# Mixing expert sizes in one group: 25 groups of four 32-place units in the first expert layer

## The chip, the cores and the metric

The kernel runs on one core of one Trainium2 chip. The metric is the device time of one execution in microseconds. Matrix products run on TensorE, element-wise work on VectorE (DVE) and ScalarE (ACT), set-up work on GpSimd (POOL), and SyncE (SP) issues nearly all DMA transfers.

## The reference, cut to what matters

Two blocks of a network follow each other on 256 rows (tokens) of 1024 numbers. Each block ends in a mixture of experts; only the first one's is touched. It has 64 experts, and every row goes to the eight with the highest scores:

```python
s = jax.nn.sigmoid((hf @ w_router).astype(jnp.float32))
_, idx = lax.top_k(s + b_router.astype(jnp.float32), TOP_K)        # TOP_K = 8 of 64
s_sel = jnp.take_along_axis(s, idx, axis=-1)
wts = s_sel / jnp.sum(s_sel, axis=-1, keepdims=True) * ROUTE_SCALE
# for the rows of each expert e, with rw the weight of row and expert:
y = (jax.nn.silu(xb @ we_gate[e]) * (xb @ we_up[e])) @ we_down[e]  # 1024 -> 256 -> 1024
acc = acc.at[rows].add(y * rw[:, None])
```

A shared expert is added for all rows. All numbers are float32, and each expert has 3 MB of weights, 1 MB for each of gate, up and down.

## The kernel before

**Groups.** The experts with numbers 0 to 3 keep places of their own, and the other 60 are sorted by their number of rows, most first, so that position 4 has most rows and position 63 fewest. A group fills the 128 output rows of TensorE with one, two or four experts of equal capacity: 128, 64 or 32 places. There are 26 groups (lines 42 to 55): the four unsorted experts by twos, then eight times one group of one or two, one of two and one of four. An expert with more rows than its capacity would be worked off by another path after the last group (`over_items`); it loads that expert's weights again.

**One group on TensorE** (`experts`, `body`, lines 1207 to 1265; the matmul helpers record lines 1215, 1228, 1246, 1251, 1361 and 1374). It is written out in this order: gate and up of group g (line 1361, for each of 8 steps over the 1024 inputs one matmul for each expert of the group; an expert's matmul uses only the columns of the array that are its places, so a group of two has tiles 128 rows by 64 columns and a group of four 128 by 32); the combine of group g-1 (line 1228, four float32 products that add the group's output rows to the tokens' rows in PSUM banks 0 to 3); transposes of the activation (line 1246) and of the weighted selection `Sw` (line 1251); the gather of group g+1 (line 1215, 48 bfloat16 products of the input, held as three bfloat16 parts, with the 0/1 selection `Sb`); down of group g (line 1374, two steps, two halves of 512 columns).

**The other engines.** VectorE makes the selection `Sb` and its weighted form `Sw` for group g+1 (lines 1974 and 1978), multiplies Silu(gate) by up (line 1990) and copies the two transposed blocks (lines 1993 and 1995). ScalarE takes Silu (line 779), copies the gathered rows (line 774), and after down copies the output rows to `Y` (line 785), which the combine waits for by the semaphore `x_Y`.

**The weights.** They come through a ring of 12 slots of 1 MB in the order in which TensorE needs them (`PIECES1`, line 60: for each group the gates, then the ups, then the downs). SP issues a piece when the piece 12 places before it has been used (line 497 waits, line 499 issues). The sorted experts' pieces also need the list of the sort, which is read before each issue. Float32 products are two records each in the trace (a weight load and a matmul, twice), bfloat16 ones one.

**What follows.** After the last combine come the norm and the second block, with a second expert layer (lines 1508 and 1520) of 8 groups of four experts, all 32 places. It shares the function `experts` and is not changed.

Of the kernel before, what the change touches and what calls it, by code (L numbers as in the profile page):

```python
# [33 lines left out]
G2 = 4  # L34
# [2 lines left out]

STATIC1 = 4  # L40
GROUPS1 = [(0, 2), (2, 2)]
_one, _two, _four = 4, 8, 32
for _t in range(8):
    if _t % 2 == 0:
        GROUPS1.append((_one, 1))
        _one += 1
    else:
        GROUPS1.append((_two, 2))
        _two += 2
    GROUPS1.append((_two, 2))  # L50
    _two += 2
    GROUPS1.append((_four, 4))
    _four += 4
assert (_one, _two, _four) == (8, 32, 64)
NG1 = len(GROUPS1)

SLOTS, SLOT_WORDS, RING0 = 12, 2048, 0
PIECES1 = [(-1, kind, 0) for kind in range(3)] + [(g, kind, j) for g, (_, n) in enumerate(GROUPS1) for kind in range(3) for j in range(n)]  # L60
# [90 lines left out]
def two_block_network(nc, A, out):  # L151
# [10 lines left out]
    with ctx:  # L162
# [136 lines left out]
        av = ce(512)  # L299
        aT = ce(4, P)  # L300
        Y = ce(D)
        mask = ce(NB, E1)
        wts = ce(NB, E1)
        rank = ce(NB, E1)
# [95 lines left out]
        def _(sp):  # L400
# [82 lines left out]
            def load_piece(i):  # L483

                g, kind, j = piece = PIECES1[i]
                slot = RING[piece][0]
                if i >= SLOTS:
                    consumed(PIECES1[i - SLOTS])
                else:

                    sp.wait_ge(S["stream_used"], AT[("adb4", "adb5", "w_out")[slot // 4]] + 1)
                if g < 0:
                    src = A[("ws_gate", "ws_up", "ws_down")[kind]][0]
                    src = rows(src) if kind == 2 else long_rows(src, KD)
                else:
                    at = GROUPS1[g][0] + j
# [162 lines left out]
        def _(act):  # L659
# [105 lines left out]
            def experts(L, NG, F, GU):  # L765
# [100 lines left out]
        def _(pe):  # L866
# [340 lines left out]
            def experts(L, NG, F, gate_and_up, down):  # L1207
                before = (L - 1) * NG1

                def gather_rows(done):  # L1210

                    for k in range(KD):
                        for q in range(NB * 3):
                            b, part = q // 3, q % 3
                            last = mm(PS[4 + k // 4][:, (k % 4) * P:(k % 4 + 1) * P], hs[:, part, b, k * P:(k + 1) * P],  # L1215
                                      Sb[:, b, :], start=(q == 0), stop=(q == NB * 3 - 1))
                        if k % 4 == 3:
                            last.then_inc(done, 1)

                def gather(n):  # L1220
                    pe.wait_ge(S["x_S"], 2 * (n + before) + 2)
                    gather_rows(S["x_gather"])

                def add_rows():

# [5 lines left out]

                def combine(g):
                    pe.wait_ge(S["x_Ct"], (g + before) + 1)
                    pe.wait_ge(S["x_Y"], 2 * (g + before) + 2)
                    return add_rows()

                def body(g, par, first=False, last=False):

                    pe.wait_ge(S["x_hTe"], 2 * (g + before) + 2)
                    gate_and_up(g)  # L1240
                    if not first:
                        combine(g - 1)

                    pe.wait_ge(S["x_act"], (g + before) + 1)
                    for f in range(F // P):
                        m = tr(PS[6][:, f * P:(f + 1) * P], av[:, f * P:(f + 1) * P], ident[:])  # L1246
                    m.then_inc(S["x_turned"], 1)
                    if first:
                        pe.wait_ge(S["over_known"], L)
                    for b in range(NB):  # L1250
                        m = tr(PS[7][:, b * P:(b + 1) * P], Sw[:, par, b, :], ident[:])
                    m.then_inc(S["x_turned"], 1)
                    if not last:
                        gather(g + 1)
# [7 lines left out]
                gather(0)  # L1262
                if L == 1:
                    shared_down()
                over_list(L)
# [85 lines left out]

            def gate_and_up1(g):

                n = GROUPS1[g][1]
                cap = P // n
                for kind in range(2):
                    for j in range(n):
                        landed((g, kind, j))
                    for k in range(KD):
                        for j in range(n):  # L1360
                            m = mm(PS[4 + kind][j * cap:(j + 1) * cap, 0:F1], hTe[:, k, j * cap:(j + 1) * cap],  # L1361
                                   piece_view((g, kind, j))[:, k, :], start=(k == 0), stop=(k == KD - 1))
                    m.then_inc(S["e1_gateup"], 1)

            def down1(g):

                n = GROUPS1[g][1]
                cap = P // n
                for j in range(n):
                    landed((g, 2, j))  # L1370
                for c in range(F1 // P):
                    for h in range(2):
                        for j in range(n):
                            m = mm(PS[6 + h][j * cap:(j + 1) * cap, :], aT[:, c, j * cap:(j + 1) * cap],  # L1374
                                   piece_view((g, 2, j))[:, c, h * 512:(h + 1) * 512], start=(c == 0), stop=(c == F1 // P - 1))
                m.then_inc(S["e1_down"], 1)

# [150 lines left out]
        def _(dve):  # L1528
# [362 lines left out]
            def over_rows(L, ne):  # L1891
# [6 lines left out]
                    step(v.memset(over_from, float(CAP2)))  # L1898
                else:

                    step(v.tensor_scalar(over_from, over_idx, 32.5, 32.0, ALU.is_lt, ALU.mult))
                    step(v.tensor_scalar(over_from, over_from, 32.0, None, ALU.add))
                    for bound, rows in ((8.5, 64.0), (4.5, -64.0)):
# [62 lines left out]
            def experts(L, NG, F, GU):  # L1966
                pre, before = f"e{L}_", (L - 1) * NG1

                def slots(n, par):

                    first, G = GROUPS1[n] if L == 1 else (n * G2, G2)
                    cap = P // G
                    for b in range(NB):
                        v.tensor_tensor(Sb[:, b, :].rearrange("p (e s) -> p e s", e=G), outer(iota[:, 0:cap], G),  # L1974
                                        inner(rank[:, b, bass.ds(first, G)], cap), ALU.is_equal).then_inc(S["x_S"], 1)
                    dve.wait_ge(S["x_S"], 2 * (n + before) + 2)
                    for b in range(NB):
                        v.tensor_tensor(Sw[:, par, b, :].rearrange("p (e s) -> p e s", e=G),
                                        Sb[:, b, :].rearrange("p (e s) -> p e s", e=G),
                                        inner(wts[:, b, bass.ds(first, G)], cap), ALU.mult).then_inc(S["x_Sw"], 1)  # L1980

                def body(g, par, last=False):
                    dve.wait_ge(S["x_Sw"], 2 * (g + before) + 2)
                    if not last:
# [5 lines left out]
                    v.tensor_tensor(av[:, 0:F].rearrange("s (c p) -> s p c", p=P), sg[:, 0:F].rearrange("s (p c) -> s p c", p=P),  # L1990
                                    PS[5][:, 0:F].rearrange("s (p c) -> s p c", p=P), ALU.mult).then_inc(S["x_act"], 1)
# [3 lines left out]
                    v.tensor_copy(Ct, PS[7][:, 0:T]).then_inc(S["x_Ct"], 1)  # L1995
# [5 lines left out]
                if L == 1:  # L2001
                    for g in range(NG):
                        body(g, g % 2, last=g == NG - 1)
                else:
                    body(0, 0)
                    with dve.Fori(0, NG // 2 - 1) as i:
# [241 lines left out]
```

## Time and profile before

| | |
|---|---|
| three runs | 1555.62, 1557.53, 1557.55 us; median 1557.53 |
| the profiled execution, first to last instruction | 1555.2 us |
| the profiled execution's time around it | no other time is shown; the span stands 2.3 us below the median of the runs |
| TensorE busy (matmul) | 1255.3 us, 81% |
| VectorE, ScalarE, GpSimd busy | 360.8, 178.9, 95.2 us |
| transfers | 507.48 MB, mean 326 GB/s |
| mean granted TensorE clock | 0.908 of full speed |
| first expert layer, first gate matmul to end of last combine | 324.5 to 810.2 us |

The profile records one execution. "Busy" counts the time in which an engine works on an instruction; TensorE matmuls overlap each other, and their ends are modelled, so starts say more than durations. The chain of waits is followed back from the last instruction: at each step to what released it, or to the instruction before it on its engine. Its pieces show what the end of the kernel hung on at each moment. "issue" is time without a wait that the profile shows.

### The profile page before, as it was taken

The page shows a single profiled execution, that of the slowest core. Times are in us where ns is not written, and L with a number is a line of the kernel's source. Part 1 is how long each engine was busy: PE and PEld are TensorE (multiplying, and loading weights), DVE is VectorE, ACT ScalarE, POOL GpSimd, SP SyncE. Part 2 cuts the span into 40 slices and gives each one's busy share as a digit, 9 for nine tenths or more (in the row PEclk, how much of TensorE's full clock was granted, in tenths as well). Part 3 has the DMA queues.
Part 4 walks back from the last instruction along what each step waited for, and adds up shares of the span by engine and source line. Part 5 has one row for each costly group of instructions (what it writes and reads, how often), then busy time and mean ns, then how long its engine had stood idle before and what let it go on. Part 6 is the DMA issues. An engine that isn't in the chain of part 4 may idle for free.

```text
span 1555.2 us, 19875 instructions
## 1 busy us (share of the span) xinstructions
PE 1255.3 (81%) x8092; PEld 644.6 (41%) x8092; DVE 360.8 (23%) x877; ACT 178.9 (12%) x340; POOL 95.2 (6%) x125
## 2 busy tenths in 40 slices
PE   4999889799989989989977988887565765765754
PEld 2763435456556556555536544433221221221211
DVE  1588452611111111111113243324000000000002
ACT  1210200311111111111110012012000000000001
POOL 2595000000000000000001000000000000000000
PEclk9999979999999999999997999998886887887787
DMA  9765992278999999999976412363999999999993
GB/s 364 274 273 212 397 413 106 97 265 320 380 420 420 420 420 421 420 421 418 421 306 221 170 47 108 145 272 123 423 421 421 421 422 421 422 422 422 422 422 141
DMA packets 83877, 507.48 MB, mean 326 GB/s; under 512 B 8262, under 2 KB 9510, under 8 KB 34260
## 3 DMA queue, kind: packets, MB, share of 16 engines
q1 hardware_dynamic: 82708, 502.98, 79.3%
q0 software_dynamic: 944, 3.29, 0.7%
q8 instruction: 58, 0.95, 0.2%
q14 instruction: 23, 0.19, 0.0%
q10 hardware_dynamic: 144, 0.07, 0.0%
HBM read 505.25 MB, written 1.06 MB: 326 GB/s over the span
## 4 chain that ended last, share of the span: by engine, by line
PE 56%; DMA 33%; DVE 6%; SPq 2%; issue 1%; ACT 1%; DVEq 0%; ACTq 0%
DMA W<-in_w_expert_down 12%; DMA W<-in_w_expert_up 10%; PE PS L1361 10%; DMA W<-in_we_up 8%; PE PS L936 5%; PE PS L1228 5%; PE PS L1374 4%; PE PS L1430 4%; PE PS L1215 3%; PE PS L1508 3%; PE PS L1520 3%; DMA W<-in_w_ada 3%; PE PS L890 2%; PE PS L1101 2%; PE PS L1390 2%; PE PS L1488 2%
## 5 line engine op out<-in xcount | busy, mean ns | idle before, releaser
L1508 PE MATMUL PS<-W,scr 128*32 128x512 f32 x1024 | 175.6, 850 | 130.6 <-DMA W<-in_w_expert_up 66.8
L1361 PE MATMUL PS<-W,scr 128*32 128x256 f32 (+2 forms) x2048 | 195.6, 399 | 24.5 <-DMA W<-in_we_up 22.7
L1990 DVE TENSOR_TENSOR scr<-scr,PS 128x256 f32<-128x256 f32 (+1 forms) x34 | 24.1, 708 | 670.5 <-PE PS L1508 387.1
L1361 PEld LDWEIGHTS PS<-W,scr 128*32 128x32 f32 (+2 forms) x2048 | 126.5, 132 | 101.7 <-issue 53.4
L1508 PEld LDWEIGHTS PS<-W,scr 128*32 128x32 f32 x1024 | 40.3, 148 | 265.1 <-issue 112.8
L1228 PE MATMUL PS<-scr 128*128 128x512 f32 x272 | 125.3, 603 | 2.6 <-ACT scr L785 2.6
L1520 PE MATMUL PS<-W,scr 128*32 128x512 f32 x512 | 71.2, 706 | 34.2 <-DMA W<-in_w_expert_down 33.2
L1215 PE MATMUL PS<-scr 128*128 128x128 bf16 x1632 | 96.7, 219 | 0.4 <-DVE scr L1974 0.4
L1374 PE MATMUL PS<-W,scr 128*32 128x512 f32 (+2 forms) x512 | 94.9, 597 | 0.7 <-DVE scr L1993 0.7
L1215 PEld LDWEIGHTS PS<-scr 128*128 128x128 bf16 x1632 | 93.9, 98 | 2.1 <-DVE scr L1945 1.2
L774 ACT COPY scr<-PS 128x512 f32<-128x512 f32 x68 | 39.9, 587 | 436.7 <-PE PS L1215 436.7
L1228 PEld LDWEIGHTS PS<-scr 128*128 128x128 f32 x272 | 49.2, 189 | 68.2 <-issue 68.0
L890 PE MATMUL PS<-W,sc 128*32 128x512 f32 x384 | 49.2, 658 | 18.1 <-DMA W<-in_w_ada 17.9
L785 ACT COPY scr<-PS 128x512 f32<-128x512 f32 x68 | 36.5, 589 | 217.9 <-PE PS L1520 125.3
L1430 PE MATMUL PS<-W,hT 128*128 128x512 f32 x128 | 57.1, 599 | 0.0
L1520 PEld LDWEIGHTS PS<-W,scr 128*32 128x32 f32 x512 | 17.6, 127 | 80.7 <-DMA W<-in_w_expert_down 40.2
L936 PE MATMUL PS<-hT,W 128*128 128x256 f32 x192 | 44.1, 392 | 4.5 <-DVE hT L1570 4.5
L1374 PEld LDWEIGHTS PS<-W,scr 128*32 128x32 f32 (+2 forms) x512 | 28.3, 126 | 47.0 <-issue 43.9
L632 POOL TENSOR_SCALAR scr<-scr,convw 128x256 f32<-128x256 f32 x44 | 44.2, 1004 | 4.3
L936 PEld LDWEIGHTS PS<-hT,W 128*128 128x128 f32 x192 | 37.6, 197 | 10.0 <-DVE hT L1570 4.6
L779 ACT ACTIVATE scr<-PS 128x256 f32<-128x256 f32 (+1 forms) x34 | 14.8, 434 | 219.9 <-PE PS L1508 142.2
L1993 DVE COPY scr<-PS 128x256 f32<-128x256 f32 (+1 forms) x34 | 16.6, 488 | 100.3 <-PE PS L1246 100.3
(411 smaller groups left out, 1111.3 us busy)
## 6 DMA issues: line engine op xcount, KB each, us to landing
W<-in_we_gate SPq DMA_DIRECT2D x64, 1024.0 KB, 19.1
W<-in_we_up SPq DMA_DIRECT2D x64, 1024.0 KB, 17.0
W<-in_we_down SPq DMA_DIRECT2D x64, 1024.0 KB, 16.0
W<-in_w_expert_gate SPq DMA_DIRECT2D x64, 1024.0 KB, 18.7
W<-in_w_expert_up SPq DMA_DIRECT2D x64, 1024.0 KB, 19.3
W<-in_w_expert_down SPq DMA_DIRECT2D x64, 1024.0 KB, 19.4
W<-in_w_ada SPq DMA_DIRECT2D x12, 4096.0 KB, 18.1
W<-in_w_in SPq DMA_DIRECT2D x6, 4096.0 KB, 14.4
```

What stands on the lines that cost most here:

```text
L632: step(g.tensor_scalar(tmp, upad[:, i, :, j:j + ROW], convw[:, 4 * j + i:4 * j + i + 1], None, ALU.mult))
L774: a.copy(hTe[:, 4 * q:4 * q + 4, :], PS[4 + q][:].rearrange("p (k s) -> p k s", k=4)).then_inc(S["x_hTe"], 1)
L785: a.copy(Y[:, h * 512:(h + 1) * 512], PS[6 + h][:]).then_inc(S["x_Y"], 1)
L890: last = mm(PS[5 + h][32 * j:32 * j + 32, :], sc[:, 2 * j + kk, 30 - row:62 - row], ada_w[n][:, 2 * j + kk, h * 512:(h + 1) * 512], start= ...
L936: last = mm(PS[bank][:, at:at + n], lhs(k), rhs(k), start=(k == 0), stop=(k == KD - 1))
L1215: last = mm(PS[4 + k // 4][:, (k % 4) * P:(k % 4 + 1) * P], hs[:, part, b, k * P:(k + 1) * P], Sb[:, b, :], start=(q == 0), stop=(q == NB ...
L1228: last = mm(PS[2 * b + h][:, :], Ct[:, b * P:(b + 1) * P], Y[:, h * 512:(h + 1) * 512], start=False, stop=False)
L1361: m = mm(PS[4 + kind][j * cap:(j + 1) * cap, 0:F1], hTe[:, k, j * cap:(j + 1) * cap], piece_view((g, kind, j))[:, k, :], start=(k == 0), s ...
L1374: m = mm(PS[6 + h][j * cap:(j + 1) * cap, :], aT[:, c, j * cap:(j + 1) * cap], piece_view((g, 2, j))[:, c, h * 512:(h + 1) * 512], start=( ...
L1430: last = mm(PS[6 + n % 2][:, :], hT[:, k, b * P:(b + 1) * P], w2k[2 + half][:, k, h * 512:(h + 1) * 512], start=(k == 0), stop=(k == KD - 1))
L1508: m = mm(PS[bank][j * CAP2:(j + 1) * CAP2, :], hTe[:, k, j * CAP2:(j + 1) * CAP2], gu2[piece][:, j, kk, :], start=(k == 0), stop=(k == KD ...
L1520: m = mm(PS[6 + h][j * CAP2:(j + 1) * CAP2, :], aT[:, c, j * CAP2:(j + 1) * CAP2], dn2[piece][:, j, cc, h * 512:(h + 1) * 512], start=(c = ...
```

## The change

The first layer's groups are built of four units of 32 places. A group is a list of (position, units): the unsorted experts keep two units each; positions 4 to 7 have three units (96 places instead of 128), 8 to 31 two and 32 to 63 one, as before. 14 groups take one expert of two units and two of one; 4 take one of three and one of one; 5, besides the first two, take two of two. That makes 25. An expert of three units is computed as a tile of 64 columns and one of 32 with the same weights (`column_tiles`).

The combine's matmuls become bfloat16: the selection's transposed form holds 0 and 1 (`CtB`), and the output rows are split into three bfloat16 parts (`Y3`) by ScalarE and VectorE in turns (`parts_of_rows`). The routing weight goes into the activation: TensorE adds up each place's weight into one column of PSUM bank 5, and VectorE's multiplication of gate and up takes it as a third factor. The selection is double-buffered (`Sb2`).

```diff
+UNIT = 32
+WIDE1, HALF1 = 8, 32
+def first_layer_groups():
+    groups = [[(0, 2), (1, 2)], [(2, 2), (3, 2)]]
+    wide, half, single = STATIC1, WIDE1, HALF1
+    for t in range(14):
+        groups.append([(half, 2), (single, 1), (single + 1, 1)])
+        half, single = half + 1, single + 2
+        if t % 3 == 1 and wide < WIDE1:
+            groups.append([(wide, 3), (single, 1)])
+            wide, single = wide + 1, single + 1
+        elif t % 3 == 2 or t == 13:
+            groups.append([(half, 2), (half + 1, 2)])
+            half += 2
+    return groups
+def column_tiles(group):
+    for j, (_, at, cap) in enumerate(places(group)):
+        for size in (2 * UNIT, UNIT):
+            if cap >= size:
+                yield j, at, size
+                at, cap = at + size, cap - size
...
 # ScalarE, experts, body
+                    if L == 1:
+                        for h in range(2):
+                            a.copy(Y3[:, 0, h * 512:(h + 1) * 512], PS[6 + h][:]).then_inc(S["x_Y"], 1)
+                        for h in range(2):
+                            act.wait_ge(S["x_rest"], 4 * g + 1 + h)
+                            a.copy(Y3[:, 1, h * 512:(h + 1) * 512], Yr[:, h * 512:(h + 1) * 512]).then_inc(S["x_Y"], 1)
+                        return
...
 # TensorE, combine
+                    pe.wait_ge(S["x_Y"], 4 * g + 4)
+                    pe.wait_ge(S["x_rest"], 4 * g + 4)
+                    for b in range(NB):
+                        for part in range(3):
+                            for h in range(2):
+                                m = mm(PS[2 * b + h][:, :], CtB[:, b * P:(b + 1) * P], Y3[:, part, h * 512:(h + 1) * 512],
+                                       start=False, stop=False)
...
 # TensorE, body
+                    if L == 1:
+                        pe.wait_ge(S["x_Sw"], 2 * g + 2)
+                        for b in range(NB):
+                            mm(PS[5][:, F:F + 1], Sw[:, par, b, :], ones[:, 0:1], start=(b == 0), stop=(b == NB - 1))
                     gate_and_up(g)
...
-                        m = tr(PS[7][:, b * P:(b + 1) * P], Sw[:, par, b, :], ident[:])
+                            m = mm(PS[7][:, b * P:(b + 1) * P], Sb2[:, par, b, :], identb, start=True, stop=True)
...
 # TensorE, gate_and_up1 (down1 likewise)
                     for k in range(KD):
-                        for j in range(n):
-                            m = mm(PS[4 + kind][j * cap:(j + 1) * cap, 0:F1], hTe[:, k, j * cap:(j + 1) * cap],
+                        for j, at, size in column_tiles(GROUPS1[g]):
+                            m = mm(PS[4 + kind][at:at + size, 0:F1], hTe[:, k, at:at + size],
                                    piece_view((g, kind, j))[:, k, :], start=(k == 0), stop=(k == KD - 1))
...
 # VectorE, body
+                        v.scalar_tensor_tensor(out=av[:, 0:F]..., in0=sg[:, 0:F]...,
+                                               scalar=PS[5][:, F:F + 1], in1=PS[5][:, 0:F]...,
+                                               op0=ALU.mult, op1=ALU.mult).then_inc(S["x_act"], 1)
...
+                def parts_of_rows(g):
+                    for h in range(2):
+                        q = slice(h * 512, (h + 1) * 512)
+                        dve.wait_ge(S["x_Y"], 4 * g + 1 + h)
+                        v.tensor_tensor(Yr[:, q], PS[6 + h][:], Y3[:, 0, q], ALU.subtract).then_inc(S["x_rest"], 1)
+                    for h in range(2):
+                        q = slice(h * 512, (h + 1) * 512)
+                        dve.wait_ge(S["x_Y"], 4 * g + 3 + h)
+                        v.tensor_tensor(Y3[:, 2, q], Yr[:, q], Y3[:, 1, q], ALU.subtract).then_inc(S["x_rest"], 1)
```

The selection on VectorE (`slots`) is made in one operation for each run of experts of equal size, so a mixed group takes two operations where a uniform one takes one, for each of two blocks and of two forms.

## Rows read from the trace of the kernel before

**Rows 1.** The page's 40 slices of 38.9 us: GB/s moved in each.

```profile
GB/s 364 274 273 212 397 413 106 97 265 320 380 420 420 420 420 421 420 421 418 421 306 221 170 47 108 145 272 123 423 421 421 421 422 421 422 422 422 422 422 141
```

**Rows 2.** Sums by stretch: busy time (and count) of each engine, clock, DMA share, GB/s.

```profile
355.00:397.00 42.00, 42.00 (x360) 26.34 (x360) 4.70 (x14) 6.72 (x13) 0.00 (x0) 1.00 0.75 289
397.00:797.00 400.00, 375.52 (x3405) 224.22 (x3394) 48.36 (x144) 55.27 (x105) 0.00 (x0) 0.97 1.01 419
```

**Rows 3.** Chain of waits, a group of two, then one of four: start, duration, what.

```profile
373.67 7.06 PE PS L1361 x64
380.72 3.63 PE PS L1228 x8
384.36 0.22 PE PS L1246 x2
...
384.79 2.68 PE PS L1215 x48
387.47 3.58 PE PS L1374 x16
391.06 7.04 PE PS L1361 x128
...
408.42 3.60 PE PS L1361 x31
```

**Rows 4.** Chain of waits where the first group begins.

```profile
324.31 0.22 PE PS L1205 x2
324.53 7.08 PE PS L1361 x64
```

**Rows 5.** Chain of waits in the last group, from its transposes on.

```profile
800.72 0.44 DVE scr L1993
...
801.57 3.67 PE PS L1374 x32
...
806.49 3.67 PE PS L1228 x8
```

**Rows 6.** Groups by form, 290 to 860 us: busy, mean ns | idle before.

```profile
L1974 DVE TENSOR_TENSOR scr<-iota,scr 128x128 bf16<-128x128 f32 x52 | 12.8, 289 | 53.2 <-PE PS L1215 53.1
...
L1882 DVE TENSOR_TENSOR xn<-PS,scr 128x512 f32<-128x512 f32 x4 | 2.5, 683 | 0.0
...
L763 ACT CAST scr<-xn 128x512 bf16<-128x512 f32 x4 | 2.4, 618 | 2.0 <-DVE xn L1882 2.0
```

**Rows 7.** TensorE timeline, last round of down and first of gate: start, duration, what.

```profile
338.69 0.60 PE L1374 MATMUL PS<-W,scr 128*64 128x512 f32 x2
339.12 0.60 PE L1361 MATMUL PS<-W,scr 128*64 128x256 f32 x4
...
390.46 0.60 PE L1374 MATMUL PS<-W,scr 128*64 128x512 f32 x2
390.99 0.42 PE L1361 MATMUL PS<-W,scr 128*32 128x256 f32 x4
...
407.81 0.61 PE L1374 MATMUL PS<-W,scr 128*32 128x512 f32 x4
408.35 0.44 PE L1361 MATMUL PS<-W,scr 128*64 128x256 f32 x2
```

**Rows 8.** TensorE timeline, the second rounds of gate after the last two borders.

```profile
391.23 0.40 PE L1361 MATMUL PS<-W,scr 128*32 128x256 f32 x4
...
408.62 0.39 PE L1361 MATMUL PS<-W,scr 128*64 128x256 f32 x2
```

**Rows 9.** TensorE timeline, down after the gather: first and second round.

```profile
387.40 0.65 PE L1374 MATMUL PS<-W,scr 128*64 128x512 f32 x2
...
387.88 0.60 PE L1374 MATMUL PS<-W,scr 128*64 128x512 f32 x2
...
404.78 0.64 PE L1374 MATMUL PS<-W,scr 128*32 128x512 f32 x4
...
405.23 0.61 PE L1374 MATMUL PS<-W,scr 128*32 128x512 f32 x4
```

More of the change, by code:

```diff
@@ L36, with places @@
 NG2 = E2 // G2
+UNIT = 32
 STATIC1 = 4
[L41 to L54, printed above, removed]
-NG1 = len(GROUPS1)
+WIDE1, HALF1 = 8, 32
[11 more added lines that the diff above has]
+            half += 2
+    assert (wide, half, single) == (WIDE1, HALF1, E1), (wide, half, single)
+    return groups
+GROUPS1 = first_layer_groups()
+NG1 = len(GROUPS1)
+def places(group):
+    start = 0
+    for position, units in group:
+        yield position, start * UNIT, units * UNIT
+        start += units
+def column_tiles(group):
[4 more added lines that the diff above has]
+                at, cap = at + size, cap - size
 SLOTS, SLOT_WORDS, RING0 = 12, 2048, 0
-PIECES1 = [(-1, kind, 0) for kind in range(3)] + [(g, kind, j) for g, (_, n) in enumerate(GROUPS1) for kind in range(3) for j in range(n)]
+PIECES1 = [(-1, kind, 0) for kind in range(3)] + [(g, kind, j) for g, group in enumerate(GROUPS1) for kind in range(3) for j in range(len(group))]
 RING = {piece: ((RING0 + i) % SLOTS, i // SLOTS) for i, piece in enumerate(PIECES1)}
@@ L301, in two_block_network @@
         Y = ce(D)
+        Y3 = ce(3, D, dt=BF16)
+        Yr = ce(D)
+        Sb2 = ce(2, NB, P, dt=BF16)
+        CtB = ce(T, dt=BF16)
+        identb = ce(P, dt=BF16)
         mask = ce(NB, E1)
@@ L1215, in gather_rows, with gather @@
                             last = mm(PS[4 + k // 4][:, (k % 4) * P:(k % 4 + 1) * P], hs[:, part, b, k * P:(k + 1) * P],
-                                      Sb[:, b, :], start=(q == 0), stop=(q == NB * 3 - 1))
+                                      pick[:, b, :], start=(q == 0), stop=(q == NB * 3 - 1))
                         if k % 4 == 3:
                             last.then_inc(done, 1)
-                def gather(n):
+                def gather(n, par):
                     pe.wait_ge(S["x_S"], 2 * (n + before) + 2)
-                    gather_rows(S["x_gather"])
+                    gather_rows(S["x_gather"], Sb2[:, par, :, :] if L == 1 else Sb)
                 def add_rows():
@@ L1250, in body @@
                     for b in range(NB):
[L1251 removed]
+                        if L == 1:
+                            m = mm(PS[7][:, b * P:(b + 1) * P], Sb2[:, par, b, :], identb, start=True, stop=True)
+                        else:
+                            m = tr(PS[7][:, b * P:(b + 1) * P], Sw[:, par, b, :], ident[:])
                     m.then_inc(S["x_turned"], 1)
                     if not last:
[L1254 removed]
+                        gather(g + 1, 1 - par)
                     pe.wait_ge(S["x_aT"], (g + before) + 1)
@@ L1261, in experts @@
                 pe.wait_ge(S["hs_left"], 8 * L)
-                gather(0)
+                gather(0, 0)
                 if L == 1:
@@ L1365, in down1 @@
             def down1(g):
-                n = GROUPS1[g][1]
-                cap = P // n
-                for j in range(n):
+                for j in range(len(GROUPS1[g])):
                     landed((g, 2, j))
@@ L1372, in down1 @@
                     for h in range(2):
-                        for j in range(n):
-                            m = mm(PS[6 + h][j * cap:(j + 1) * cap, :], aT[:, c, j * cap:(j + 1) * cap],
+                        for j, at, size in column_tiles(GROUPS1[g]):
+                            m = mm(PS[6 + h][at:at + size, :], aT[:, c, at:at + size],
                                    piece_view((g, 2, j))[:, c, h * 512:(h + 1) * 512], start=(c == 0), stop=(c == F1 // P - 1))
@@ L1899, in over_rows @@
                 else:
-                    step(v.tensor_scalar(over_from, over_idx, 32.5, 32.0, ALU.is_lt, ALU.mult))
-                    step(v.tensor_scalar(over_from, over_from, 32.0, None, ALU.add))
-                    for bound, rows in ((8.5, 64.0), (4.5, -64.0)):
+                    step(v.tensor_scalar(over_from, over_idx, HALF1 + 0.5, float(UNIT), ALU.is_lt, ALU.mult))
+                    step(v.tensor_scalar(over_from, over_from, float(UNIT), None, ALU.add))
+                    for bound, rows in ((WIDE1 + 0.5, float(UNIT)), (STATIC1 + 0.5, -float(UNIT))):
                         step(v.tensor_scalar(cap_tmp, over_idx, bound, rows, ALU.is_lt, ALU.mult))
@@ L1969, in slots @@
                 def slots(n, par):
-                    first, G = GROUPS1[n] if L == 1 else (n * G2, G2)
-                    cap = P // G
+                    if L == 1:
+                        parts = []
+                        for first, at, cap in places(GROUPS1[n]):
+                            if parts and parts[-1][3] == cap and parts[-1][0] + parts[-1][1] == first:
+                                parts[-1][1] += 1
+                            else:
+                                parts.append([first, 1, at, cap])
+                    else:
+                        parts = [[n * G2, G2, 0, CAP2]]
+                    pick = Sb2[:, par, :, :] if L == 1 else Sb
                     for b in range(NB):
-                        v.tensor_tensor(Sb[:, b, :].rearrange("p (e s) -> p e s", e=G), outer(iota[:, 0:cap], G),
-                                        inner(rank[:, b, bass.ds(first, G)], cap), ALU.is_equal).then_inc(S["x_S"], 1)
+                        for first, G, at, cap in parts:
+                            ins = v.tensor_tensor(pick[:, b, at:at + G * cap].rearrange("p (e s) -> p e s", e=G), outer(iota[:, 0:cap], G),
+                                                  inner(rank[:, b, bass.ds(first, G)], cap), ALU.is_equal)
+                        ins.then_inc(S["x_S"], 1)
                     dve.wait_ge(S["x_S"], 2 * (n + before) + 2)
                     for b in range(NB):
-                        v.tensor_tensor(Sw[:, par, b, :].rearrange("p (e s) -> p e s", e=G),
-                                        Sb[:, b, :].rearrange("p (e s) -> p e s", e=G),
-                                        inner(wts[:, b, bass.ds(first, G)], cap), ALU.mult).then_inc(S["x_Sw"], 1)
+                        for first, G, at, cap in parts:
+                            ins = v.tensor_tensor(Sw[:, par, b, at:at + G * cap].rearrange("p (e s) -> p e s", e=G),
+                                                  pick[:, b, at:at + G * cap].rearrange("p (e s) -> p e s", e=G),
+                                                  inner(wts[:, b, bass.ds(first, G)], cap), ALU.mult)
+                        ins.then_inc(S["x_Sw"], 1)
                 def body(g, par, last=False):
@@ L2001, in experts @@
                 if L == 1:
+                    step(v.tensor_copy(identb, ident[:]))
                     for g in range(NG):
                         body(g, g % 2, last=g == NG - 1)
+                        parts_of_rows(g)
                 else:
```

24 lines of the change are left out of this document (14 added, 10 removed).

## The prediction

> **What bounds the kernel now.** I read the 40 slices of the page first, then sums by stretch over the first expert layer, then the chain of waits at its start, in its middle and at its end, and last single tensor matmuls where one tile width follows another. The 40 slices show two stretches at 420 GB/s, one in each expert layer [rows 1]. In the first layer, 324.5 to 810 us, the sums by stretch show that from 397 to 797 the weights stream at 419 GB/s, while TensorE is busy 375.5 of 400 us; from 355 to 397 TensorE is busy all the time and the DMAs move only 289 GB/s [rows 2]. So the layer is bound by TensorE for its first 70 us and by the stream of weights after that, but TensorE has little to spare: the chain gives one group of experts 17.4 us (373.67 to 391.06, and 391.06 to 408.42), whatever its number of experts [rows 3]. It is the reserve that this change spends: 26 groups of 17.4 us are 452 us of the 485 us that the layer takes.
>
> **The parts of a group.** In the chain a group is: gate and up 7.05, combine 3.63, four transposes 0.44, gather 2.68, down 3.58 [rows 3].
>
> Combine. Four float32 products of 512 columns (8 records, 3.63) become twelve bfloat16 ones. The gather is 48 bfloat16 records of 128 columns, 6144 columns in 2.68 us; twelve of 512 are 6144 columns too: 2.68. Minus 0.95.
>
> Turning the selection. Two float32 transposes of the weights (0.22) become two bfloat16 products of 128 columns, 2/48 of the gather's time (0.11). Minus 0.1.
>
> Weight per row. Two new float32 products with one column are 4 records with 128x128 weights each. One such product of 36 columns, 2 records, takes 0.22 us in the chain just before the first group [rows 4], so two take 0.44. They also put full-width work between two tiled stages, which costs a change of width more (below, 0.10). I take plus 0.6; the ends are 0.4 and 0.9.
>
> The multiplication on VectorE reads one more scalar. It stands beside the combine, and what waits for it (the transposes) stands behind the combine on TensorE anyway: it costs nothing up to 2.68 us, and the VectorE operations of up to 128x512 take 0.3 to 0.7 us [rows 6]. In the first group, without a combine, it could cost 0.1. The copies of the transposed blocks stand beside the gather as before: 0. So does the one new conversion of the identity, once. The loads come in another order on SP, each with its wait and its issue as before, 192 of them: 0 while the ring is full.
>
> Three parts of the rows. In the last group down ends at 805.24 (801.57 + 3.67) and the combine starts at 806.49, 1.25 us for two halves copied by ScalarE [rows 5]. Now it is copy, subtract, cast, subtract, in halves. Neighbours: a subtraction of 128x512 from PSUM 683 ns, a bfloat16 cast 618 ns [rows 6]. Pipelined over halves it is about 0.6+0.7+0.7+0.6+0.7 with waits, 3.9 us. Combine comes after the next group's gate and up (7 us), so in the 24 inner places it is covered. Behind it on VectorE stands the next selection, up to 8 operations of at most 0.29 us [rows 6]: 3.9+2.3 is 6.2, still below 7, and the up product is awaited anyhow. TensorE's combine has a longer wait, for the subtractions too, and behind it are the transposes into the banks that these read; both come after it anyway. On ScalarE the next Silu stands behind the casts; it needs the next gate, 3.5 us later, and can be 0 to 1 us late, under cover of up. Only the last group pays: 3.9 instead of 1.25, plus 2.7.
>
> Sum for a group of one tile width: 17.4 - 0.95 - 0.1 + 0.6 = 16.95 us.
>
> **The mixed groups.** 18 of the 25 groups (14 of three experts, 4 with a 96-place one) issue, for each of 8 steps of gate and of up, a 64-wide tile and two 32-wide tiles, and so for each of 4 steps of down. Before, a group has tiles of one width only. The trace shows what a change of width costs at stage borders. From 64 to 64 wide, the last 512-column round starts at 338.69 and the next stage at 339.12: 0.43, the length of the round. From 64 to 32 wide it is 390.46 to 390.99, from 32 to 64 wide 407.81 to 408.35, thus 0.53 and 0.54 [rows 7]. A change costs 0.10 us, in either direction. The first round after it is longer as well: a 256-column round starts its follower after 0.24 (390.99 to 391.23, 32 wide) or 0.27 (408.35 to 408.62, 64 wide) [rows 8], where 32 rounds in 7.05 us are 0.22 each; of 512 columns, 387.40 to 387.88 is 0.48 and 404.78 to 405.23 is 0.45 [rows 9], against 0.43. No new-width matmul starts while one of the old width runs. That is the point: four tiles of one width share a round (four 32-wide ones start within it), but here every round would hold one width.
>
> I take it that the new width waits for the old one's end even where the columns are disjoint. Each float32 product is two rounds. One step of gate or up is then 64 wide 0.27 + 0.22 + 0.10 minus rounding (0.58), 32 wide 0.24 + 0.22 + 0.10 minus rounding (0.55): 1.13 us instead of 0.43. Sixteen steps: 18.1 instead of 6.9, plus 11.2. One step of down: 0.48 + 0.53 + 0.45 + 0.53 less rounding, 1.98 instead of 0.86; four steps: 7.9 instead of 3.5, plus 4.4. A mixed group takes 16.95 + 15.6 = 32.55 us.
>
> Its bounds: below, the widths overlap at no cost (plus 0); above, the passes alternate between the widths, eight changes a step pair instead of four, 1.25 us a step and 20 us for gate and up, 8.4 for down: plus 18, 35 us.
>
> The Trainium skill, TensorEngine Tiling (Array Packing), Key Properties, says the same more strongly: changing the tiling mode, not just the tile, drains the engine. The 0.10 us agrees, and a drain means no overlap of the two widths; the trace has no pair of widths on disjoint columns, so no row shows that half. By the rule the sum is the one above; without it, it would be that of the first rival.
>
> **Sum of the layer.** 18 x 32.55 = 585.9, 7 x 16.95 = 118.7, together 704.6. The first group has no combine of its predecessor (-2.7), the last gathers nothing (-2.7) and waits 0.9 for its transposed rows (800.72 to 801.57 [rows 5]), and then come 3.9 and the last combine 2.7: 706.7 us. From 324.53 [rows 4] the layer ends at 1031, where the last combine ended at 810.2 before [rows 5]: plus 221. The weights don't hold this up: three experts are 9 transfers of 1.05 MB, 22.5 us at 419 GB/s [rows 2], below 32.55, and the ring of 12 pieces is refilled a group ahead. What follows (the block after it, the second expert layer, whose code is unchanged) moves back as a whole. The profiled execution's span is 1555.2 us, 2.3 below the median of 1557.53; I add the difference to the median: 1557.5 + 221 = 1778.5, rounded to 1778 us.
>
> **Rivals.**
> 1. Faster: widths on disjoint columns share the array and a change costs nothing. For it: tiles of one width do run side by side, four 32-wide ones in the time of one. Against it: the 0.10 us at every change. Then every group takes 16.95, and the stream binds. The first sorted groups hold three experts instead of one, two and four, so the ring is emptied sooner: the stretch 355 to 397 was short of 419 GB/s by 130 x 42 us = 5.5 MB, 5.2 transfers or 13 us [rows 2]. Less 2.7 for the longer tail: minus 10, 1547 us. It holds as long as TensorE is faster than the stream: 180 sorted transfers at 2.5 us are 450 us, less 118.7 for the seven others leaves 18.4 us for each mixed group. Its own ends are 0 and minus 13, without the tail.
> 2. Little change, slower by about 1%: a change costs its 0.10 us and the slower first round, but disjoint tiles overlap. A step is 0.43 + 0.20 + 0.05, 0.68 us; gate and up 10.9, down 4.4: plus 4.9, 21.8 a mixed group. 18 x 21.8 + 118.7 = 511, plus 2.1, from 324.5 to 838: plus 27, 1585 us. It sits between one and the forecast.
> 3. The new chain of four steps is the bound (VectorE or ScalarE late for combine in each group). By the sum above it is 6.2 of 7 us; if it took 9, 7 unmixed groups would lose 2 us each and, without the slow mixed tiles, hidden behind the stream. It is worth at most 14 us and needs rival 1 to be seen.
> 4. It doesn't do what it says: an expert beyond 96 places would go the overflow way. That way loads the expert again; the sign of it would be more transfers of gate weights than there are experts; each such expert would add a whole pass of gather, gate, up and down after the last group, 17 us and its loads, and the prediction would be short by that.
>
> **Chances.** Forecast 0.82, rival 1 0.10, rival 2 0.05, the rest 0.03. The forecast's own range is 1745 to 1850: 18 groups at 31 to 36 us. For other splits of the rounds I widen it downwards, to 1690 to 1850. A measurement of this kernel can tell 0.2% (3 us) from no change: faster 0.09, within it 0.03, slower 0.88.
>
> **What would show it.** Gate and up of a mixed group at 18 us and down at 8 in the chain, starts of 64- and 32-wide matmuls never in one round; the share of DMA in the chain of the first layer gone and its rate near 300 GB/s; combine 2.7 us, ready before gate and up end; unmixed groups at 17 us. It is wrong if mixed gate and up stays near 7 us with DMA waits as before.

## The result and the profile after

The changed kernel takes 1777.35 us (median of 4 runs, 1775.53 to 1778.05), the kernel before 1556.6 (4 runs); the ratio is 1.1411, 95% interval 1.1397 to 1.1424. The forecast was 1778 us. The profiled execution took 1777.13 us with a span of 1775.4, 220.2 more than the span before.

The chain of waits through the second group (two experts, one width) and the third (three experts, two widths); start, duration, what. L1412 is gate and up, L1279 combine, L1296 the first transposes, L1252 gather, L1423 down, L1289 the weight for each row:

```profile
341.81 0.54 PE PS L1289 x4
342.35 7.06 PE PS L1412 x64
...
349.56 2.54 PE PS L1279 x11
...
355.11 3.58 PE PS L1423 x16
358.69 0.54 PE PS L1289 x4
359.23 18.11 PE PS L1412 x96
...
377.50 2.54 PE PS L1279 x11
380.03 0.22 PE PS L1296 x2
...
380.36 2.68 PE PS L1252 x48
383.04 7.94 PE PS L1423 x24
390.98 0.54 PE PS L1289 x4
```

They answer to [rows 3]. A group of one width lasts 16.88 us (341.81 to 358.69), a mixed one 32.29 (358.69 to 390.98). Gate and up of the mixed group take 18.11 us for 96 records; the uniform group of four before took 7.04 for 128.

The TensorE timeline of the first steps of that gate shows why. Each row is a query of a short window (20 to 130 ns) that begins after one start, so the row's start is that of the earliest matmul still running, and its count includes any that start within the window:

```profile
359.16 0.43 PE L1412 MATMUL PS<-W,scr 128*64 128x256 f32 x1
...
359.43 0.38 PE L1412 MATMUL PS<-W,scr 128*64 128x256 f32 x1
...
359.74 0.62 PE L1412 MATMUL PS<-W,scr 128*32 128x256 f32 x4
...
359.98 0.39 PE L1412 MATMUL PS<-W,scr 128*32 128x256 f32 x2
...
360.29 0.43 PE L1412 MATMUL PS<-W,scr 128*64 128x256 f32 x1
```

The 64-wide product's two rounds start at 359.16 and 359.43, the first round of the two 32-wide products at 359.74, their second at 359.98, the next 64-wide one at 360.29. No round holds both widths, although their columns are disjoint; the intervals are 0.27, 0.31, 0.24 and 0.31, together 1.13 us a step. (This goes by starts. The modelled end of the 64-wide round, 359.43 + 0.38, lies 0.07 us behind the next start, as the ends do at the borders in [rows 7].)

Sums by stretch (busy time and count of each engine, clock, DMA share, GB/s), to be held against [rows 2]:

```profile
355.00:397.00 42.00, 41.84 (x239) 14.70 (x238) 8.94 (x27) 6.73 (x12) 0.00 (x0) 1.00 0.76 300
397.00:797.00 400.00, 397.77 (x2469) 154.82 (x2481) 67.97 (x186) 51.72 (x95) 0.00 (x0) 1.00 0.71 280
```

The stream of weights no longer binds: 280 GB/s where it was 419, and TensorE is busy 397.8 of 400 us. The end of the layer, to be held against [rows 5]:

```profile
1018.84 3.67 PE PS L1423 x16
1022.53 0.59 ACT scr L816
1023.15 0.70 DVE scr L2068
1023.87 0.62 ACT scr L819
1024.52 1.30 DVE scr L2072 x2
...
1025.96 4.44 PE PS L1279 x12
1030.40 1.81 issue
1032.20 0.40 PE PS L1359
```

Where the 220.2 us are: the layer, from its first gate to the end of the last combine, lasts 703.3 us (327.10 to 1030.40) instead of 485.6, plus 217.7. 2.1 came before it, nearly all of it where the chain's first product of the kernel took 5.65 us instead of 3.69, in code that isn't touched. 0.4 is the first weight column. From the end of the last combine on both need 745.0 us; the 1.81 us of issue behind the combine are within that, and smaller differences later make up for them.

### The profile page after: what moved, and what is told of

The parts are those of the page before. It is cut to its first block, busy times and chain, and to the rows that moved or that the text cites. A ratio compares the mean times of both kernels' runs of the same rounds, so it can differ in the third digit from the quotient of the medians.

```text
span 1775.4 us, 20664 instructions
## 1 busy us (share of the span) xinstructions
PE 1497.3 (84%) x8368; PEld 647.0 (36%) x8392; DVE 427.9 (24%) x1043; ACT 206.7 (12%) x385; POOL 95.2 (5%) x125
## 4 chain that ended last, share of the span: by engine, by line
PE 70%; DMA 22%; DVE 5%; issue 1%; SPq 1%; ACT 1%; DVEq 0%; ACTq 0%
PE PS L1412 21%; DMA W<-in_w_expert_down 10%; PE PS L1423 9%; DMA W<-in_w_expert_up 9%; PE PS L973 5%; PE PS L1252 4%; PE PS L1279 4%; PE PS L1479 3%; PE PS L1557 3%; PE PS L1569 2%; DMA W<-in_w_ada 2%; PE PS L927 2%; PE PS L1138 2%; PE PS L1439 2%; PE PS L1537 2%; PE PS L1522 2%
## 5 line engine op out<-in xcount | busy, mean ns | idle before, releaser
L1412 PE MATMUL PS<-W,scr 128*32 128x256 f32 (+1 forms) x2176 | 377.1, 392 | 0.0
L1412 PEld LDWEIGHTS PS<-W,scr 128*32 128x32 f32 (+1 forms) x2176 | 128.0, 121 | 237.5 <-issue 222.0
L1423 PE MATMUL PS<-W,scr 128*64 128x512 f32 (+1 forms) x544 | 169.7, 607 | 0.8 <-DVE scr L2059 0.8
L804 ACT COPY scr<-PS 128x512 f32<-128x512 f32 x66 | 38.7, 587 | 478.1 <-PE PS L1252 478.1
L1252 PE MATMUL PS<-scr 128*128 128x128 bf16 x1584 | 93.8, 219 | 0.0
L1252 PEld LDWEIGHTS PS<-scr 128*128 128x128 bf16 x1584 | 90.1, 98 | 1.4 <-DVE scr L1994 0.8
L2068 DVE TENSOR_TENSOR scr<-PS,scr 128x512 f32<-128x512 f32 x50 | 32.2, 686 | 232.8 <-ACT scr L816 232.8
L2052 DVE SCALAR_TENSOR_TENSOR scr<-scr,PS 128x256 f32<-128x256 f32 x25 | 16.8, 670 | 283.1 <-PE PS L1412 283.1
L1423 PEld LDWEIGHTS PS<-W,scr 128*64 128x64 f32 (+1 forms) x544 | 31.7, 121 | 118.9 <-issue 115.5
L1279 PE MATMUL PS<-scr 128*128 128x512 bf16 x276 | 65.3, 386 | 7.3 <-issue 3.8
L1569 PEld LDWEIGHTS PS<-W,scr 128*32 128x32 f32 x512 | 17.4, 127 | 79.8 <-DMA W<-in_w_expert_down 39.2
L816 ACT CAST scr<-PS 128x512 bf16<-128x512 f32 x50 | 26.9, 589 | 161.1 <-PE PS L1423 161.1
L1279 PEld LDWEIGHTS PS<-scr 128*128 128x128 bf16 x300 | 27.7, 99 | 44.5 <-issue 15.7
```

What stands on the lines that cost most here:

```text
L804: a.copy(hTe[:, 4 * q:4 * q + 4, :], PS[4 + q][:].rearrange("p (k s) -> p k s", k=4)).then_inc(S["x_hTe"], 1)
L1279: m = mm(PS[2 * b + h][:, :], CtB[:, b * P:(b + 1) * P], Y3[:, part, h * 512:(h + 1) * 512], start=False, stop=False)
L1412: m = mm(PS[4 + kind][at:at + size, 0:F1], hTe[:, k, at:at + size], piece_view((g, kind, j))[:, k, :], start=(k == 0), stop=(k == KD - 1))
L1423: m = mm(PS[6 + h][at:at + size, :], aT[:, c, at:at + size], piece_view((g, 2, j))[:, c, h * 512:(h + 1) * 512], start=(c == 0), stop=(c = ...
L1569: m = mm(PS[6 + h][j * CAP2:(j + 1) * CAP2, :], aT[:, c, j * CAP2:(j + 1) * CAP2], dn2[piece][:, j, cc, h * 512:(h + 1) * 512], start=(c = ...
```

## The experiments

**All tiles 32 wide.** The change with one function altered:

```diff
-        for size in (2 * UNIT, UNIT):
-            if cap >= size:
-                yield j, at, size
-                at, cap = at + size, cap - size
+        while cap > 0:
+            yield j, at, UNIT
+            at, cap = at + UNIT, cap - UNIT
```

> All tiles of the first expert layer are 32 wide (an expert of 64 places is two tiles with the same weights), the rest of the change stays. Theory (two widths never share a round, and each change of width costs about 0.1 us more): gate and up of every group 7.1 us, down 3.6, a group 16.9 us of TensorE; then the stream of weights binds and the kernel takes about 1547 us (1543 to 1557), near or below the kernel before. Rival (the mixed groups are slow because a step has more matmuls and weight loads, three or more for a group, and issue can't keep up): four tiles a step are worse than three, gate and up 18 us or more, about 1777 us or above.

Measured: ratio to before 0.9995 (0.9984 to 1.0007), median 1555.62 us. A group of three experts in its chain, from its weight column to the next one's:

```profile
356.24 0.54 PE PS L1288 x4
356.78 7.04 PE PS L1411 x128
...
369.53 3.57 PE PS L1422 x32
373.10 0.54 PE PS L1288 x4
```

128 records take 7.04 us, 96 took 18.11. A query of the timeline inside its first round shows four 32-wide matmuls running together, where the changed kernel has one of 64 and then two of 32:

```profile
356.71 0.42 PE L1411 MATMUL PS<-W,scr 128*32 128x256 f32 x4
```

More matmuls and more weight loads cost nothing as long as they share rounds; the loss of 220 us is gone. The forecast of 1547 for this case was too low, see below.

**Widths apart.** The changed kernel with the same products in another order, all 64-wide ones of a stage first (down likewise):

```diff
+                    for width in widths(GROUPS1[g]):      # 64, then 32
                     for k in range(KD):
                         for j, at, size in column_tiles(GROUPS1[g]):
+                            if size != width:
+                                continue
```

> In a mixed group all 64-wide matmuls of gate come first, then all 32-wide ones; up and down likewise. Each product is the same, only their order changes: 2 changes of width a stage instead of 16. Theory: what is lost to sharing stays, 2 x 8 x 0.43 = 6.9 us a stage, and the changes fall to about 0.2: gate and up 14.2 us instead of 18.1, down 7.1 instead of 7.9; a mixed group 27.6 us, the layer 18 x 4.7 = 85 us shorter than in the changed kernel, about 1693 us. If widths on disjoint columns can run side by side and only the change itself is dear: gate and up near 8 us here, and the kernel near 1550. If the change costs nothing and only sharing is lost: 1777 less almost nothing.

Measured: 1693.72 us, ratio 1.0881 (1.0859 to 1.0903). The third group in its chain:

```profile
358.81 0.54 PE PS L1294 x4
359.35 14.35 PE PS L1420 x96
...
379.40 7.13 PE PS L1434 x24
386.54 0.54 PE PS L1294 x4
```

It splits the cost. In gate and up 28 of 32 changes of width went, and 3.76 us with them: 0.13 for each change, its 0.10 and the longer first round. The other 7.3 us of the 11 (14.35 against 7.06) stayed: each stage still needs 16 rounds of one width and then 16 of the other. This run prices the two parts. It does not test whether two widths could overlap, because here a 64-wide matmul has a 32-wide one beside it only at the borders of the blocks; that is read from the starts in the changed kernel, where the two follow each other at every step.

**One tile less.** In each mixed group the last 32-wide tile is left out, so that its expert isn't computed:

```diff
                         for j, at, size in column_tiles(GROUPS1[g]):
+                            if size == UNIT and at == 3 * UNIT:
+                                continue
```

> The last of the two 32-wide tiles of each mixed group is left out in gate, up and down (its expert is not computed). Theory: the two 32-wide tiles shared their rounds, so one alone takes the same: gate and up 18.1 us, down 7.9, 1777 us within 3. Rival (cost goes by the number of matmuls): a third less, gate and up 12 us, about 1620 us.

One run: 1771.58 us, span 1769.8. The third group in its chain:

```profile
357.38 18.00 PE PS L1414 x64
...
381.08 7.91 PE PS L1427 x16
389.00 0.54 PE PS L1289 x4
```

64 records take 18.00 us where 96 took 18.11: the time goes by the rounds, not by the matmuls. The total is 5.6 us of span lower, more than expected; 0.14 us in each of 18 groups is 2.5 of it, 1.9 lie before the third group, and the gap of 1.81 at the end isn't there; the three together are 6.2, slightly more than the difference.

**The kernel before with mixed pairs.** Nothing of the change but the two widths, in the groups of two:

```diff
-                        for j in range(n):
+                        for j, at, size in tiles(n):      # n == 2: (0, 0, 64), (1, 64, 32), (1, 96, 32)
```

> The kernel before, groups and arithmetic untouched; only the second expert of each of its 13 groups of two is computed as two 32-wide tiles instead of one 64-wide. Theory: nothing but the two widths makes the time: gate and up 18.1 us and down 7.9 in these 13 groups, 33 us each instead of 17.4, the other 13 stay at 17.4; TensorE binds throughout (655 us), the layer ends 169 us later, about 1726 us. Rival (the dearness belongs to groups of three experts or to the new combine and its waits): gate and up stay near 7.1 us, and 1557.

Measured: 1739.9 us, ratio 1.1174 (1.1152 to 1.1197). The groups of two last 32.8 us, here the second one in the chain:

```profile
354.50 18.11 PE PS L1367 x96
372.61 3.63 PE PS L1228 x8
...
379.36 7.94 PE PS L1380 x24
387.30 7.10 PE PS L1367 x32
```

The 14 us above the expected 1726 are my count: there are 14 groups of two and 12 others, not 13 and 13, and 14 x 32.8 + 4 x 17.1 + 8 x 17.4 is 667 us (the trace: 665.9). The mechanism needs neither three experts in a group nor the new combine.

**The rest of the change alone, with the 26 old groups.** The edit, shortened (`one`, `two` are counters):

```diff
-    for t in range(14):
-        groups.append([(half, 2), (single, 1), (single + 1, 1)])
+    for t in range(8):
+        groups.append([(one, 4)] if t % 2 == 0 else [(two, 2), (two + 1, 2)])
+        ...
```

> The 26 groups of the kernel before with the rest of the change: bfloat16 combine of three parts, routing weight in the activation. Theory: a group takes 0.5 us less of TensorE (16.9 for 17.4), which shows only in the first 4 or 5 groups, before the stream of weights binds (minus 2 us); the tail is 2.7 us longer, and the last combine runs at the lower clock (up to 2 more): 1555 to 1560 us, no difference that can be told. Rival (the new chain of copy, subtract, cast, subtract is late for each combine): several us for each group, 1570 us or more.

Measured: 1559.34 us, ratio 1.0013 (1.0002 to 1.0025). TensorE's 0.5 us a group bring nothing: in the profile the last ups start at 790.36, before at 790.50. The layer ends 2.9 us later there (813.10 against 810.16), since the chain after down is 2.2 us longer and the last combine took 5.28 us, at a granted clock of 0.50, instead of 3.67. The 2 us that the first groups were to give are not seen.

**The new groups alone, all tiles 32 wide, with the old combine.** The kernel before with the new lists and `column_tiles` as in the first experiment.

> The kernel before with the new 25 groups, all tiles 32 wide; the float32 combine with the weighted selection, as before. Theory: the stream of weights binds as in the kernel with all tiles 32 wide and the new combine. A group takes 17.4 us of TensorE instead of 16.9 in the first four (plus 2 us), the tail has two float32 combines (plus 2.2) and a chain after down that is 2.2 us shorter: the layer ends 0 to 2 us after that kernel's, thus 1550 to 1557. If the three bfloat16 parts are what matters for the time: 5 us or more slower than that kernel.

Measured: 1551.25 us, ratio 0.9958 (0.9943 to 0.9974): a little faster than before (6 runs, the interval is clear of 1), and 0.23 to 0.37% (4 to 6 us) below the two ratios of the same groups with the new combine, 0.9995 and, from the next run, 0.9981. The interval of the second (0.9971 to 0.9990) just overlaps this one. Its last combine, in the chain from the copies after down:

```profile
801.98 0.47 ACT scr L809
...
802.46 0.60 ACT scr L809
...
803.20 3.67 PE PS L1252 x8
806.87 0.23 PE PS L1330
```

**The first experiment again, for where its gain went.**

> The kernel with all tiles 32 wide once more, to see whether its layer really ends 6 us earlier. Its profiled execution (1547.8 us of span) was 7.4 us shorter than that of before, but the median of its runs only 0.8 us. If the gain in the first layer holds in each execution and something later takes it back, this profile ends the first layer at 804 again with a longer remainder; if executions differ in the first layer itself, the layer's end moves.

Measured: 1553.75 us, ratio 0.9981 (0.9971 to 0.9990). The same kernel gave 0.9995 in the first set of runs, so two sets of one kernel can differ by 0.14%, 2 us. Its layer's end:

```profile
802.18 2.10 PE PS L1278 x9
804.28 4.23 issue
808.51 0.62 PE PS L1358
```

Executions differ at the layer's end itself. The combine is over at 804.28, as in the first profile (803.73), but TensorE's next matmul, for which the profile shows no wait on data, comes 4.23 us later instead of 0.

**The next block's loads held back.** In the kernel with all tiles 32 wide, SP issues them only when the layer is summed:

```diff
-            with sp.If(count > 0):
-                sp.wait_ge(S["y_done"], 4)
+            sp.wait_ge(S["y_done"], 4)
```

> The kernel with all tiles 32 wide and the bfloat16 combine; the next block's first weights (4 MB and two of 1 MB) are issued only when the layer's sums are complete, 6 us later than before, not when the last down is. In its two profiles TensorE's step from the last combine to the closing matmuls took 0.23 and 4.23 us with the DMAs at 415 GB/s. Theory (TensorE fetches its next instructions there, and these transfers stand behind the weights): with idle DMAs the step is 0.2 us in each execution, and the median falls by 2 to 4 us to about 1551. Rival (the step's length has nothing to do with the transfers): no change, 1554 to 1556, or slower where the 4 MB come late for the block's first matmul.

Measured: 1553.24 us, ratio 0.9978 (0.9966 to 0.9990), not told apart from the kernel without the wait (0.9981 and 0.9995). In its one profile the next matmul came 0.43 us after the combine, but the median did not fall to the expected 1551: the transfers are not shown to be the cause of the gap, and the theory gets no support. In that profile the last combine was slow with the DMAs idle (clock 0.64, 6 GB/s):

```profile
803.00:807.20 4.20, 4.17 (x12) 1.37 (x12) 0.00 (x0) 0.00 (x0) 0.00 (x0) 0.64 0.02 6
```

The same edit in the kernel with the new groups and the old combine:

> The same wait in the kernel with the new groups, all tiles 32 wide, and the old float32 combine. Its step took 0.23 us in its profile, the weights having started only 3.7 us before. Theory: there is nothing to gain, 1551 within 2 us; it is slower only if the 4 MB, issued 5 us later, are late for the first matmul of the next block (16 us after the issue before).

Measured: 1550.01 us, ratio 0.9954 (0.9939 to 0.9970), as expected nothing gained beyond the 0.9958 without the wait.

**TensorE kept busy before the last combine.** In the kernel with all tiles 32 wide and the new combine:

```diff
+                if L == 1:
+                    for _ in range(14):
+                        mm(PS[4][:, :], zeros[:, 0:P // 2].bitcast(BF16), outer(ones[:].bitcast(BF16), 2), start=True, stop=True)
                 combine(NG - 1).then_inc(S["over_done"], 1)
```

> The kernel with all tiles 32 wide and the bfloat16 combine; 14 bfloat16 matmuls of 512 columns on zeros (3 us), whose result nobody reads, fill TensorE's wait of 3.5 us between the last down and the last combine of the layer. In four of six profiles with that wait the last combine ran at the lower of the two clock levels (4.2 to 5.2 us instead of 2.7). Theory (the idle stretch brings the clock down): the last combine takes 2.7 us at the full clock here, and the median is about 1.5 us below that of the kernel without the filling (0.9995 and 0.9981 of before), near 0.997. Rival (the level falls by chance of when the chip looks, or the weights' transfers matter): the combine is slow here as often, and the median stays or is worse by the filling.

Measured: 1550.88 us, ratio 0.9963 (0.9952 to 0.9974). The last combine and the step behind it:

```profile
804.05 2.75 PE PS L1278 x12
806.80 0.23 PE PS L1361
```

The combine runs at the full clock (1.00 in the stretches from 797.5 to 808). But this does not show the theory: both profiles of the same kernel without the filling also have their last combine at the full clock, 2.75 us each, behind 3.5 us of idle TensorE. The slow ones are in other kernels and in the run with the loads held back. The ratio is below both of the same kernel without the filling; its interval just overlaps that of 0.9981 and is clear of that of 0.9995. Whether the filling gains anything, and whether by the clock or by the missing gap, stays open.

## Why the prediction was right, by its steps

- **Bound.** The reserve of TensorE (17.4 us a group against the stream) was the quantity that decided. Right.
- **Parts of a group.** A uniform group was put at 16.95 us and is 16.88: combine 2.69 from the end of gate and up to the transposes (377.34 to 380.03; 2.68 forecast), the weight column 0.54 (0.6), the turned selection 0.11 (0.11). VectorE's product is 0.67 us instead of 0.61, hidden. The new chain in four steps was never late before the last group.
- **Mixed groups.** 18.11 and 7.94 us against 18.1 and 7.9; a group 32.29 against 32.55. This was worked out from borders between stages alone ([rows 7 to 9]), which showed 0.10 us for a change of width and a longer first round but no pair on disjoint columns. The step taken on trust, that disjoint columns don't help, is now shown by the starts in the timeline: four of one width together (356.71), never one width beside the other. The kernel before with mixed pairs has the same 18.11 and 7.94 us, and with one tile less the time stays at 18.00, so neither the rest of the change nor the number of matmuls makes it. The widths apart give the two prices, 3.8 us for the changes and 7.3 us for the rounds. This is what the Trainium skill's TensorEngine Tiling (Array Packing), Key Properties, calls a drain at a change of mode; the trace agrees in both halves, 0.10 us and no overlap.
- **Sum of the layer.** 706.7 us forecast, 703.3 measured. The mixed groups were 4.7 us too dear (18 x 0.26), the last combine 1.7 too cheap (4.44 for 2.7, at the lower clock, which the sum had left out), the chain before it 3.5 instead of 3.9. That the total came out within 1 us of the median is in part luck: 2.1 us from the start of the kernel happened to fill the rest. The forecast's own range was written a little wider than its terms: 18 groups at 31 to 36 us give 1750 to 1840, not 1745 to 1850.
- **Rival 1, faster.** Its condition was false in the changed kernel and is true in the first experiment, so its price could be measured: not minus 10 but minus 1 to minus 3. Its first profile shows the parts, sums by stretch and then the last up in its chain:

```profile
355.00:397.00 42.00, 41.68 (x594) 24.11 (x592) 14.12 (x42) 10.36 (x19) 0.00 (x0) 1.00 0.99 400
...
780.00:800.00 20.00, 16.27 (x199) 7.94 (x192) 5.75 (x10) 4.85 (x9) 0.00 (x0) 1.00 0.38 149
...
786.38 3.66 PE PS L1411 x64
```

  The last up of the kernel before, in its chain:

```profile
790.50 6.33 PE PS L1361 x64
```

  The stream starts as early as claimed (400 GB/s where it was 289) and ends some 10 us earlier. But the layer doesn't end with the stream: TensorE's chain after the last awaited ups follows. Before, four downs followed the last group's ups, now two, so these ups came only 4.1 us earlier (786.38, before 790.50). The term of 13 us was taken at the wrong transfer. The layer of this profile ends 6.4 us earlier. The other 2.3 us: the last up took 6.33 us before, at a granted clock of 0.57 after 3.5 us of idle TensorE, and takes 3.66 here, at 1.00 after 0.3 us (minus 2.7); two new combines save 1.9; the longer tail costs 2.2.

  In the other five profiles with the new groups at one width (both combines) the last awaited transfer lies earlier still, at the ups of the group before the last. Here the second profile of the same kernel:

```profile
768.39 5.35 PE PS L1411 x64
...
783.55 7.04 PE PS L1411 x128
```

  From 768.39 on, 35.9 us of TensorE's chain without a wait for weights end the layer, the last group's gate and up among them. In all six the layer ends 3.0 to 6.7 us before 810.2. Why the median of the first experiment is only 0.8 us below is not shown: its profiled execution was the fastest of ten (1549.62 us, the others up to 1559.08), so this profile doesn't stand for the median.
- **Rivals 2 to 4.** The widths do not overlap, the chain of four is covered, and there were 64 transfers of gate weights, so no expert overflowed.
- **Signs.** The rate in the layer was put near 300 GB/s and was 280 from 397 to 797; DMA waits are gone from the layer's chain.

## What to carry to other kernels

In all these runs 64- and 32-wide column tiles share rounds only with tiles of their own width. To pack 64 and 32 places in one group, split the 64 into two 32-wide tiles with the same weights: more instructions, no time (7.04 us for gate and up). Before making an engine cheaper in a stage bound by a stream, ask at which transfer the stage really ends. With the groups alone and one width the kernel is 0.4% faster than before (0.9958), and no run shows a gain from the new combine beside them.

## What the runs showed that I had not expected

- The last combine waits 3.5 us for the chain of copy and subtract, with TensorE idle, and in five of the seven profiles with that wait it then took 4.2 to 5.3 us instead of 2.7. The two others, both of the first experiment's kernel, have the same wait and 2.75 us, so an idle stretch of this length does not always bring the clock down. In the changed kernel the granted clock is 1.00 from 1022 to 1026 and 0.61 from 1026 to 1030, so most of that stretch is at the lower level, 1.2 of 2.4 GHz:

```profile
1022.00:1026.00 4.00, 0.53 (x5) 0.07 (x2) 2.58 (x4) 2.29 (x4) 0.00 (x0) 1.00 0.54 191
1026.00:1030.00 4.00, 4.00 (x12) 1.37 (x12) 0.00 (x0) 0.00 (x0) 0.00 (x0) 0.61 1.02 417
```

  With the float32 combine TensorE is idle there for 1.3 us, and the combine took 3.67 us in each of its four profiles. Kept busy, the bfloat16 one took 2.75 in its one profile. The lower clock follows waits for weights as well: the last up before (790.50, after 3.5 us idle, clock 0.57) and that of the group before the last above (768.39, 5.35 us, after 3.8 us idle, clock 0.68).
- Behind the last bfloat16 combine TensorE's next matmul came 0.0, 0.43, 1.81 or 4.23 us later, without a wait on data. In the 4.23 us the trace has two transfers of instructions on queues beside the weights at 414 GB/s. Holding the weights back didn't change the median beyond the noise, so the cause of the gap is open.
